# Three rounded passes in place of full-precision matmuls in the state-space half of the branch units and in the output projection, with the low parts made by GpSimd

## What is computed

```
(sc_b, sc_c, sc_x, q, k, v, z, xbc, dt_raw, gl_a, gl_b, gl_c) = split_columns(h @ w_in)
y_a = short_conv_mixer(...) @ w_sc_out          # 256 -> 1024
y_b = stick_breaking_attention(...) @ w_sb_out  # 256 -> 1024
y_c = mamba2_mixer(...) @ w_ssm_out             # 512 -> 1024
merged = sigmoid(gl_a) * y_a + sigmoid(gl_b) * y_b + sigmoid(gl_c) * y_c
mix_out = merged @ w_o                          # 1024 -> 1024
x = x + gate1 * rms_norm(mix_out, g_post_mix)
h2 = rms_norm(x, g_pre_ffn) * (1 + scale2) + shift2
x = x + gate2 * rms_norm((silu(gt) * up) @ w_ffn_out, g_post_ffn)   # gt, up = h2 @ w_ffn_in
```

## Time and profile before

| what | value |
|---|---|
| median of three runs | 1241.84 us (1240.37 to 1242.09) |
| time of the profiled execution | 1236.98 us |
| its span (first to last instruction) | 1235.1 us |
| mean granted TensorE clock | 0.972 of full speed |
| TensorE matmul busy | 1105.8 us (90%) |
| VectorE / ScalarE / GpSimd busy | 860.3 / 482.1 / 468.4 us |
| stage of the `br` and `wo` units | 212 us to 269 us from the span's start |

### The profile page before, as it was taken

One profiled execution on the slowest core, in us unless ns is written; L12 is line 12 of the kernel. 1 busy time (PEld: TensorE's weight loads), 2 busy tenths in 40 slices (PEclk: granted clock), 3 DMA queues, 4 the chain that ended last, 5 costly groups with the idle time before them and its releaser, 6 DMA issues.

```text
span 1235.1 us, 14335 instructions
## 1 busy us (share of the span) xinstructions
PE 1105.8 (90%) x4768; PEld 728.9 (59%) x4768; DVE 860.3 (70%) x1923; ACT 482.1 (39%) x1121; POOL 468.4 (38%) x360
## 2 busy tenths in 40 slices
PE   4999999999999998999899999987877878778776
PEld 3999899749999998875555655423323323223222
DVE  6684567546898888737787847758668486685555
ACT  2226242044333335534544344433434334325344
POOL 0243333023544552303354455643544534444420
PEclk9999999999999998999999999998898998999999
DMA  9757665564767874564999999999999999999994
GB/s 382 289 204 265 259 260 201 208 238 171 291 282 282 335 300 176 207 259 166 421 407 423 421 420 421 422 422 421 422 421 421 422 421 422 421 421 422 421 421 190
DMA packets 57802, 413.05 MB, mean 334 GB/s; under 512 B 6544, under 2 KB 6544, under 8 KB 8208
## 3 DMA queue, kind: packets, MB, share of 16 engines
q0 software_dynamic: 41328, 296.24, 58.2%
q1 hardware_dynamic: 16272, 115.83, 23.9%
q10 hardware_dynamic: 144, 0.26, 0.1%
HBM read 411.26 MB, written 1.05 MB: 334 GB/s over the span
## 4 chain that ended last, share of the span: by engine, by line
PE 58%; DMA 29%; DVE 8%; ACT 3%; issue 1%; POOL 1%; SPq 0%; ACTq 0%; DVEq 0%; POOLq 0%
PE ps L1085 14%; PE ps L519 7%; PE ps L520 7%; PE ps L521 7%; DMA gate_area<-in_experts,idx 6%; DMA areas_seam<-in_experts,idx 6%; DMA spare<-in_experts,idx 6%; PE ps L560 5%; PE ps L506 4%; DMA mod_ring<-in_experts,idx 3%; DMA ring<-in_experts,idx 3%; DMA ring<-in_experts,part_buf 2%; PE ps L780 2%; PE ps L626 2%; DMA areaB<-in_mod_w 2%; PE ps L486 1%
## 5 line engine op out<-in xcount | busy, mean ns | idle before, releaser
L1464 ACT ACTIVATE act<-now 128x1 f32<-128x1 f32 x256 | 50.7, 198 | 265.3 <-DVE now L2308 262.7
L1085 PE MATMUL ps<-areaB,mod_sum 128*128 128x512 f32 x232 | 117.4, 639 | 23.6 <-ACT mod_sum L1472 23.6
L1561 POOL TENSOR_TENSOR w_lo<-ring,w_hi 128x512 fp32r<-128x512 f32 x41 | 98.4, 2415 | 56.4 <-ACT w_hi L1227 56.3
L1750 DVE SCALAR_TENSOR_TENSOR mod_sum<-mod_ring,cols,mod_sum 128x256 f32<-128x256 f32 x280 | 118.8, 500 | 0.0
L1618 POOL DMA_INDIRECT areaB<-in_experts,idx x58 | 66.1, 1139 | 121.4 <-PE ps L1085 61.0
L1472 ACT ACTIVATE mod_sum<-small,act 128x128 f32<-128x128 f32 x256 | 102.8, 402 | 16.0 <-ACT act L1468 0.4
L1085 PE MATMUL ps<-ring,mod_sum 128*128 128x512 f32 x192 | 94.8, 626 | 15.8 <-ACT mod_sum L1472 15.3
L1761 DVE TENSOR_TENSOR w_lo<-ring,w_hi 128x1536 fp32r<-128x1536 f32 x41 | 91.3, 2251 | 22.4 <-ACT w_hi L1227 22.3
L1227 ACT ACTIVATE w_hi<-ring 128x2048 fp32r<-128x2048 f32 x41 | 78.4, 1913 | 55.7 <-DMA ring<-in_stream 45.6
L519 PE MATMUL ps<-hT_h,w_lo 128*128 128x256 f32 x352 | 98.4, 279 | 0.8 <-DVE hid_l L1988 0.8
L521 PE MATMUL ps<-hT_h,w_hi 128*128 128x256 f32 x352 | 98.2, 279 | 0.0
(11 more groups left out here) (428 smaller groups left out, 2525.2 us busy)
## 6 DMA issues: line engine op xcount, KB each, us to landing
ring<-in_stream SPq DMA_DIRECT2D x75, 1024.0 KB, 6.0
mod_ring<-in_mod_w POOLq DMA_DIRECT2D x24, 1024.0 KB, 6.0
mod_ring<-in_mod_w SPq DMA_DIRECT2D x18, 1024.0 KB, 5.8
gate_area<-in_mod_w SPq DMA_DIRECT2D x3, 1024.0 KB, 13.2
areaB<-in_mod_w SPq DMA_DIRECT2D x3, 1024.0 KB, 23.1
gate_area<-in_stream SPq DMA_DIRECT2D x3, 1024.0 KB, 13.1
small<-in_small SPq DMA_DIRECT2D x1, 1352.0 KB, 28.6
x_sb<-in_x SPq DMA_DIRECT2D x1, 1024.0 KB, 8.9
```

Source lines behind the costliest of these rows:

```text
L1085: last = mm(ps[:, B3 + 2 * b + t, :], spread_w[n // FEW % 2][:, n % FEW, :], row[ROW_OF[n]][:, D + 512 * b:D + 512 * b + 512], start=first ...
L1561: nc.gpsimd.tensor_tensor(w_lo[s][:, HALF:], slot[s][:, HALF:], w_hi[s][:, HALF:].bitcast(F32), ALU.subtract).then_inc(lo_pool, 1)
L1750: ins = V.scalar_tensor_tensor(out=o[n], in0=w, scalar=vec[:, k:k + 1], in1=o[n], op0=ALU.mult, op1=ALU.add)
```

## The change

The 8 fp32 matmuls of each `br` unit for `yc`, and all matmuls of the four `wo` units, become `mm3` triples. For that

- ScalarE copies the high part of `yc`, of the second half of each `br` unit and of each `wo` unit (in two halves): 1 + 4 + 8 instructions of 128 x 1024. `yc` and `br` 0 and 1 come between the copies of `gl` 10 and `gl` 11, the others behind `gl` 11 and ahead of the two row copies.
- GpSimd subtracts: again 1 + 4 + 8 instructions of 128 x 1024, one input from `yc` or the ring, one the high part. The result is written over the unit in the ring. The loads of modulation units 26 and 27 come between `br` 1 and `br` 2, those of 28 and 29 behind `wo` 3.
- VectorE writes the merged activations as a high part (`hT_h`, which lies in `mT`) and a low part (`hT_l`, which lies in `hT`): per unit a rounded sum, the same sum unrounded, and their difference, where one sum stood.
- TensorE waits for `front_lo_ready` ahead of each triple block: in each `br` unit once, in `wo` tile 0 once per half unit.

```diff
@@ -63,6 +63,7 @@
 SPLITS = AT["wo2", 1] - SPLIT0
 HALF = 3 * UNIT // 4
 FRONT0, FRONT1 = AT["sc", 1], AT["gl", 11] + 1
+FRONTS = FRONT1 - FRONT0
 
 MODS = 48
 MOD_EARLY = 8
@@ -268,6 +270,12 @@
         w_lo = [rounded(f"w_lo{s}", "areaB", s * UNIT, UNIT) for s in range(RING)]
         front_hi = [rounded(f"front_hi{n}", "spare", n * UNIT // 2, 2, UNIT // 4) for n in range(2)]
         front_lo = [rounded(f"front_lo{n}", "xn", n * UNIT // 2, 2, UNIT // 4) for n in range(2)]
+        ring_lo = [rounded(f"ring_lo{s}", "ring", s * UNIT, UNIT) for s in range(RING)]
+        yc_h, yc_l = rounded("yc_h", "areaA", 2048, 4, T), rounded("yc_l", "areaA", 3072, 4, T)
+        br_hi = [rounded(f"br_hi{j}", *at, UNIT // 2)
+                 for j, at in enumerate((("areaB", 6144), ("areaB", 7168), ("spare", 0), ("spare", 1024)))]
+        wo_hi = [rounded(f"wo_hi{j}", *at, UNIT)
+                 for j, at in enumerate((("xn", 0), ("areaA", 5656), ("areaB", 6144), ("areaA", 0)))]
         hq_h, hq_l = rounded("hq_h", "mT", 0, 4, T), rounded("hq_l", "mT", 4 * T, 4, T)
         hT_h, hT_l = rounded("hT_h", "mT", 0, KC, T), rounded("hT_l", "hT", 0, KC, T)
 
@@ -600,15 +608,21 @@
                 for h in range(2):
                     broadcast_half(n, h)
 
-            def wide(kind, j, lhs):
-
-                w = arrived(kind, j)
-                bank = B3 + 2 * (j // 2)
+            def wo_tile(j, t):
+
+                both = wo_hi[j], ring_lo[AT["wo", j] % RING]
+                for k in range(4):
+                    kk = 4 * (j % 2) + k
+                    if t == 0 and k % 2 == 0:
+                        pe.wait_ge(front_lo_ready, FRONTS + 1 + 4 + 2 * j + k // 2 + 1)
+                    last = mm3(ps[:, B3 + 2 * (j // 2) + t, :], [v[:, kk, t * P:(t + 1) * P] for v in hT_parts],
+                               [v[:, 512 * k:512 * k + 512] for v in both], kk == 0, kk == KC - 1)
+                return last
+
+            def wide(j):
+
                 for t in range(NT):
-                    for k in range(4):
-                        kk = 4 * (j % 2) + k
-                        last = mm(ps[:, bank + t, :], lhs[:, kk, t * P:(t + 1) * P], w[:, 512 * k:512 * k + 512],
-                                  start=(kk == 0), stop=(kk == KC - 1))
+                    last = wo_tile(j, t)
                 last.then_inc(unit_done, 1)
 
 
@@ -774,26 +788,29 @@
                 w = arrived("br", j)
                 banks = (3, 4, 5) if j % 2 == 0 else (6, 7, 0)
                 at = 0
-                for n, (y, kc) in enumerate(((ya, 2), (yb, 2), (yc, 4))):
+                for n, y in enumerate((ya, yb)):
                     for b in range(2):
-                        for k in range(kc):
-                            last = mm(ps[:, banks[n], b * T:(b + 1) * T], w[:, at:at + P], y[:, k, :],
-                                      start=(k == 0), stop=(k == kc - 1))
+                        for k in range(2):
+                            mm(ps[:, banks[n], b * T:(b + 1) * T], w[:, at:at + P], y[:, k, :],
+                               start=(k == 0), stop=(k == 1))
                             at += P
+                pe.wait_ge(front_lo_ready, FRONTS + 1 + j + 1)
+                both = br_hi[j], ring_lo[AT["br", j] % RING][:, UNIT // 2:]
+                for b in range(2):
+                    for k in range(4):
+                        at = (4 * b + k) * P
+                        last = mm3(ps[:, banks[2], b * T:(b + 1) * T], [v[:, at:at + P] for v in both],
+                                   [v[:, k, :] for v in (yc_h, yc_l)], k == 0, k == 3)
                 last.then_inc(unit_done, 1)
             pe.wait_ge(merged, 3)
-            wide("wo", 0, mT)
+            wide(0)
             pe.wait_ge(merged, 4)
             broadcast_half(0, 0)
-            wide("wo", 1, mT)
+            wide(1)
             broadcast_half(0, 1)
             for t in range(NT):
-                for j in range(2):
-                    w = arrived("wo", 2 + j)
-                    for k in range(4):
-                        kk = 4 * j + k
-                        last = mm(ps[:, B3 + 2 + t, :], mT[:, kk, t * P:(t + 1) * P],
-                                  w[:, 512 * k:512 * k + 512], start=(kk == 0), stop=(kk == KC - 1))
+                for j in range(2, 4):
+                    last = wo_tile(j, t)
                     if t == 1:
                         last.then_inc(unit_done, 1)
                 if t == 0:
@@ -1231,6 +1248,19 @@
                 act.wait_ge(w_in[u % RING], 16 * (u // RING + 1))
                 act.wait_ge(unit_done, u - 1)
                 A(front_hi[u % 2], second_half(u), ACT.Identity).then_inc(front_hi_ready, 1)
+
+            def split_br(j):
+
+                u = AT["br", j]
+                act.wait_ge(w_in[u % RING], 16 * (u // RING + 1))
+                A(br_hi[j], slot[u % RING][:, UNIT // 2:], ACT.Identity).then_inc(front_hi_ready, 1)
+
+            def split_wo(j):
+
+                u = AT["wo", j]
+                act.wait_ge(w_in[u % RING], 16 * (u // RING + 1))
+                for half in (slice(0, UNIT // 2), slice(UNIT // 2, UNIT)):
+                    A(wo_hi[j][:, half], slot[u % RING][:, half], ACT.Identity).then_inc(front_hi_ready, 1)
 
             def half_copy(n, h, half):
                 act.wait_ge(row_mm, 2 * n + h + 1)
@@ -1309,6 +1339,18 @@
                 if j == 9:
                     act.wait_ge(yms, 1)
                     A(ysq[:, 0:2, :], ysq[:, 0:2, :], ACT.Sqrt).then_inc(yroot, 1)
+                if j == 10:
+                    act.wait_ge(yc_ready, 1)
+                    A(yc_h, yc, ACT.Identity).then_inc(front_hi_ready, 1)
+                    split_br(0)
+                    split_br(1)
+            split_br(2)
+            split_br(3)
+            split_wo(0)
+            split_wo(1)
+            act.wait_ge(unit_done, DONE("br", 1))
+            split_wo(2)
+            split_wo(3)
             row_copy(0, gate_halves)
             act.wait_ge(merged, 4)
             split_hi(SPLIT0)
@@ -1545,7 +1587,31 @@
             nc.gpsimd.tensor_tensor(hq_l, hT[:, 4:KC, :], hq_h.bitcast(F32), ALU.subtract).then_inc(hq_lo_ready, 1)
             for u in range(FRONT0, FRONT1):
                 split_front(u)
-            load_mods(MOD_SP, MOD_FRONT + 2)
+            load_mods(MOD_SP, MOD_SP + 2)
+
+            def split_output(m, low, source, high):
+
+                pool.wait_ge(front_hi_ready, FRONTS + m + 1)
+                nc.gpsimd.tensor_tensor(low, source, high.bitcast(F32), ALU.subtract).then_inc(front_lo_ready, 1)
+
+            def split_br(j):
+                s = AT["br", j] % RING
+                split_output(1 + j, ring_lo[s][:, UNIT // 2:], slot[s][:, UNIT // 2:], br_hi[j])
+
+            def split_wo(j):
+                s = AT["wo", j] % RING
+                for h, half in enumerate((slice(0, UNIT // 2), slice(UNIT // 2, UNIT))):
+                    split_output(5 + 2 * j + h, ring_lo[s][:, half], slot[s][:, half], wo_hi[j][:, half])
+
+            split_output(0, yc_l, yc, yc_h)
+            split_br(0)
+            split_br(1)
+            load_mods(MOD_SP + 2, MOD_SP + 4)
+            split_br(2)
+            split_br(3)
+            for j in range(4):
+                split_wo(j)
+            load_mods(MOD_SP + 4, MOD_FRONT + 2)
 
             def load_mod(m, i=0):
 
@@ -1966,7 +2032,11 @@
                 step.wait()
                 step(V.tensor_tensor(pr[0], pr[0], pr[1], ALU.add))
                 step.wait()
-                V.tensor_tensor(mT[:, 2 * j:2 * j + 2, :], pr[0], pr[2], ALU.add).then_inc(merged, 1)
+                high = hT_h[:, 2 * j:2 * j + 2, :]
+                step(V.tensor_tensor(high, pr[0], pr[2], ALU.add))
+                step(V.tensor_tensor(pr[0], pr[0], pr[2], ALU.add))
+                step.wait()
+                V.tensor_tensor(hT_l[:, 2 * j:2 * j + 2, :], pr[0], high.bitcast(F32), ALU.subtract).then_inc(merged, 1)
             mod_units(26, MOD_FRONT)
 
             split_lo(SPLIT0)
```

More of the change, by code:

```diff
@@ L122, in sb @@
         def sb(name, n, dt=F32):
-            start[name] = nc.sbuf_base
+            start[name] = -(-nc.sbuf_base // 32) * 32
             return ctx.enter_context(nc.sbuf_tensor(name, [P, n], dt))
@@ L145, in build @@
         mod_ring = sb("mod_ring", 2 * UNIT)
+        assert start["mod_ring"] == start["ring"] + 4 * RING * UNIT
         gate_area = sb("gate_area", 24 * T)
```

## The result

The changed kernel takes 1244.57 us (median of 22 runs, 1239.45 to 1249.35) against 1241.29 us of the kernel before in the same comparison (22 runs, 1237.47 to 1245.44): a ratio of 1.0029 with a 95% interval of 1.0018 to 1.0039, that is 2.2 to 4.8 us slower. The forecast was 4.4 us slower.

What follows compares the result with a forecast made beforehand. TensorE's chain was taken to bound the stage, savings counting only if `gu` 0's load, ScalarE and VectorE follow. 3.0 us late plus 1.4 for clock gave 4.4 on 1236.98, 1241.4; with 4.86 to the median, 1246.2 us; range 1237 to 1251.

Steps and rivals of the forecast that it cites:

- TensorE's own saving: In `br` and `wo` units: 0.41 us saved per `br` unit, 1.36 per `wo` unit, together 7.0 us without waits.
- The exclusion: GpSimd subtractions and VectorE instructions with two SBUF inputs never run together; whichever comes second waits.
- The series of units 24 and 25: VectorE's series for modulation units 24 and 25, delayed by subtractions, ends near 220.4 us instead of 213.7.
- The wait before `br` 2: TensorE needs `merged` 1 at 225.1 us but gets it at 228.9: a wait of 3.8 us.
- The wait of 2.8 us before `br` 3: `br` 2 ends at 235.4 us, but `merged` 2 comes only at 238.2, so TensorE waits 2.8.
- `merged` 2 = 228.9 + 4.65 + two subtractions of `wo` 0: VectorE's sums of `br` 1, 4.65 us, are crossed by two GpSimd subtractions and end at 238.2.
- `merged` 4 is at 250.0, hidden: VectorE's last sum of `br` 3 comes at 250.0 us while `wo` 0 runs to 250.7, costing no wait.
- 3.0 us late into the feed-forward: At the stage's end, the norm's delay, put at 2.6 or 3.5 us, is taken as 3.0 and passed on whole.
- 1.4 us for the clock: TensorE's new waits bring one stretch of lower clock, costing 1.4 us, bounds 0 and 5.
- Rival A: TensorE's saving comes through, `merged` keeps its slack: 7.0 us less about 1.0 for `wo` 3's low parts, 1235.8; chance 0.20.
- the landing of `gu` 0: Behind `wo` 1: a TensorE saving counts only if this load, ScalarE's work behind it and VectorE come forward too.
- its sentence on `spread` and the two series: Sign of being right: VectorE's `spread` and its series of units 24 and 25 come some 6 us later.

Runs made afterwards that it cites:

- run 1: Changed kernel without GpSimd's 13 subtractions; ScalarE writes zeros as low parts, products with those low parts left out; 1239.29 us, ratio 0.9982 to the kernel before.
- run 4: Changed kernel with all 13 subtractions made by VectorE, in its own order, instead of GpSimd; 1238.57 us, ratio 0.9982 to the kernel before.
- run 5: run 4 with the loads of modulation units 28 and 29 held back until `gu` 0 has landed; 1236.51 us, ratio 0.9959 to the kernel before.
- run 2: Also called `collide_only`: kernel before with 13 GpSimd subtractions added on data nobody uses, loads of units 24 to 29 split as in the change; 1241.59 us, ratio 1.0004.
- run 6: run 5 with the norm taken ahead of `gu` 0's split on ScalarE and VectorE; 1236.04 us, ratio 0.9962 to the kernel before.
- wo_dve_hold: Changed kernel with `br` units in fp32, `wo` low parts by VectorE, loads of units 28 and 29 held back; 1239.27 us, ratio 0.9982 to the kernel before.
- wo_only: Changed kernel with `br` units back in fp32, leaving GpSimd's eight subtractions for the `wo` units; 1238.55 us, ratio 0.9981 to the kernel before.
- br_only: Changed kernel with `wo` units back in fp32, five GpSimd subtractions and VectorE's old sums; 1240.43 us, ratio 0.9993 to the kernel before.

## Why the prediction was right, and where it was not

**TensorE's own saving** was sized rightly: a `br` unit took 6.32 us (216.38 to 222.70) where 6.5 had been reckoned, and `wo` 0's 24 instructions came every 0.23 us. **The exclusion** of the earlier trace rows was the mechanism: run 1 takes it away and the loss goes, to a gain.

**The series of units 24 and 25** was put at 220.4 instead of 213.7, 6.7 us late: it ended 7.8 us after `br` 0's start, where it ended 1.7 before, 6.1 late. **The wait before `br` 2** was put at 3.8 us: 3.50. These two hold.

**The wait of 2.8 us before `br` 3** failed: no wait. The step behind it was "`merged` 2 = 228.9 + 4.65 + two subtractions of `wo` 0", and those came too late to collide. The load of `wo` 0, issued at 229.2 when TensorE had ended `br` 1, took 7.3 us and not the 4.8 of the earlier trace rows: the DMA engines were busy throughout (0.97 of the time from 228 to 233) with this load and those of units 26 and 27, which VectorE's late series had put off to 224.4. The forecast had that delay, but not what it does to the load beside them. GpSimd began on `wo` 0 at 237.69, and VectorE's four sums of `br` 1 were over at 237.2, 0.69 us each. The low clock isn't needed for this: at full speed `br` 2 would have ended near 239.0 (232.69 + 6.32), still behind `merged` 2. It did make `br` 2 take 9 us instead of 6.5. The collisions fell on the sums of `br` 3 instead, where I had written **"`merged` 4 is at 250.0, hidden"**: it came 3.44 us too late for the broadcast. Two of three statements on waits hold in size, and the second wait is in the wrong place.

**"3.0 us late into the feed-forward"** and **1.4 us for the clock**: together 4.4, against 5.7 in the profiled pair, whose 5.7 includes the clock. The size of the clock's term was wrong for this execution. It had 6.8 us at the lower level around the end of the first wait (0.81 of full speed from 229.0 to 232.7, 0.70 from 232.7 to 241.7) and 3.4 behind the second; some 1.4 of these fell into the wait itself, and the rest at half speed is about 4.4 us of TensorE's work. An estimate up to the end of `wo` 1: waits 3.50 + 3.44, clock 4.4, less a saving of 2.4 in the `br` units (4 x 0.59) and 2.7 in two `wo` units, is 6.2 us late; measured were 6.7 (`wo` 1 ended 49.1 us after `br` 0, before 42.4), where the forecast had 2.7.

So the mechanism was right, and the closeness of the sum (4.4 forecast, 3.3 between the medians) is in part luck: a wait that wasn't there, one that wasn't seen, and a clock term at a third of what this execution shows. The medians of 22 runs lie 3.3 us apart, so the usual execution loses less than this pair. How much of the 3.3 is the clock's was not separated: no run changes the clock alone.

**Rival A failed as it was priced**, though run 1 and run 4 meet its condition. I gave it "7.0 us less about 1.0". With no wait for VectorE before `br` 2 the gain was 2.2 and 2.2 us. What its price left out is the landing of `gu` 0: I had said at the start that it must come forward with TensorE, and then didn't price it. In run 4 the load was issued 3.0 us earlier than before (39.4 us after `br` 0, not 42.4) and landed hardly earlier. The loads of units 28 and 29 used to be issued 4 to 5 us ahead of it (249.62 and 250.30, against 254.45); now they run beside `gu` 0 from the start, whose 1 MB took 8.4 to 9.0 us. Run 5 gives 2.9 us more (0.9982 to 0.9959).

**What I would have missed without run 2**: that the collisions cost by themselves nothing that can be measured. My working charged each of them to `merged`; rightly, since I had also lengthened VectorE's work, but the forecast doesn't say that the loss needs both, and as worded its sentence on `spread` and the two series would have let one expect a loss of 3 us and more from run 2. In the kernel before, `merged` 1 was ready 3.4 us ahead of its use, and VectorE had 3.6 us idle in front of each unit; two sums more and two subtractions per unit are 1.3 + 4.6.

## What to carry to other kernels

Work given to GpSimd isn't free because GpSimd is idle: where it reads SBUF and VectorE's instruction has two inputs there, the two take turns (and in these runs VectorE's TENSOR_SCALAR with one tile from SBUF took turns too), and GpSimd's turn is twice as long as VectorE would need for the same subtraction (2.36 against 1.23 us for 128 x 1024). Add up the time that both want between two deadlines and compare it with the slack; here the same subtractions made by VectorE in an order of its own turned 0.3% slower into 0.2% faster. And when a stage gets shorter, look at what it then meets: holding back two loads that nobody was waiting for gave another 0.2%, and this version with 1236.5 us, and run 6 with 1236.0, were the best complete ones.

## What was not expected of the hardware

- **Who gets in.** In the front of the kernel before, five of GpSimd's 20 subtractions waited for the end of a VectorE series and took 3.5 to 5.5 us; others fell into a series and got in. In the changed stage none waited: all 13 took 2.35 to 2.6 us (for those of a `wo` unit, the mean of its two), and in `collide_only` a series of 14 instructions was stretched from 5.6 to 14.09 us by four of them. The Trainium skill (SBUF — State Buffer, "Who interferes with whom") has the loser wait for one instruction of the winner; the changed stage's rows agree (a sum of 0.69 us took 2.83 across one subtraction of 2.45), and those at 187.88 us, with 5.48 us for one subtraction, don't. What decides was not found.
- **A load beside others.** `gu` 0's 1 MB landed after 4.84 us alone in run 5, and after 8.35 to 8.96 beside two other loads of 1 MB. In run 4 the DMA engines moved 410 to 426 GB/s from 256 to 262 us; three megabytes at that rate take 7.4 us (an estimate), so nearly all of the difference is the others' bytes. Alone isn't always 4.84, though: in `wo_dve_hold` it took 6.41, and why was not found.
- **The clock behind the norm.** The kernel before had 3.4 us at the lower level behind the norm. Runs 1, 4, 5 and 6 and `wo_only`, whose last tile of the norm came 0.3 to 5.4 us sooner, had 10.2 us; but so had the kernel before with only the norm moved, and the changed kernel, where that tile came 5.7 us later (0.53 of full speed from 282 to 293 us), and `br_only`, with the tile 2.1 us sooner, had 3.4. So these profiles show no tie between the length of the stretch and the time of the norm; one profile shows one draw.
